# The depthwise convolution on TensorE: two 64-row units a tile, or sets of four 32-row matmuls

## What is computed

```
def conformer_conv_module(h, w_pw1, b_pw1, w_dw, b_dw, ln_g, ln_b, w_pw2, b_pw2):
    a = jnp.einsum("bsd,de->bse", h, w_pw1) + b_pw1
    u = a[..., :d] * jax.nn.sigmoid(a[..., d:])
    u = causal_dwconv(u, w_dw, b_dw)
    u = jax.nn.silu(layernorm(u, ln_g, ln_b))
    return jnp.einsum("bsd,de->bse", u, w_pw2) + b_pw2
```

## Time and profile before

| | us |
|---|---|
| median of 3 runs (949.39 to 950.07) | 949.61 |
| the profiled execution | 950.07 |
| its span | 948.3 |
| TensorE busy in it | 938.4 |
| VectorE busy | 552.4 |
| ScalarE busy | 393.4 |
| POOL busy | 112.2 |

### The profile page before, as it was taken

How to read it: one execution, slowest core, us unless ns; L and a number is a source line. 1 busy time by engine, 2 the same in 40 slices (tenths; PEclk the granted TensorE clock), 3 DMA queues, 4 the chain that set the end, 5 groups by cost and what they waited for, 6 DMA issues and landing times.

```text
span 948.3 us, 11921 instructions
## 1 busy us (share of the span) xinstructions
PE 938.4 (99%) x4512; PEld 791.2 (83%) x4512; DVE 552.4 (58%) x703; ACT 393.4 (41%) x606; POOL 112.2 (12%) x74
## 2 busy tenths in 40 slices
PE   8999999999999999999999999999999999999997
PEld 6889899888888888888888898888888888888887
DVE  6899995657555555555434359765555655532333
ACT  7785596434333333332222355433333333322231
POOL 0558896000000000000000020000000000000000
PEclk9999999999999999999999999999999999999999
DMA  7320022233222222312232341233222232223212
GB/s 254 116 89 1 1 90 89 90 99 110 102 88 88 88 88 97 123 63 91 76 107 91 117 147 55 89 108 113 88 88 88 88 94 100 64 90 122 91 62 90
DMA packets 17020, 88.56 MB, mean 93 GB/s; under 512 B 2016, under 2 KB 4320, under 8 KB 9952
## 3 DMA queue, kind: packets, MB, share of 16 engines
q1 hardware_dynamic: 16416, 87.67, 27.2%
q10 hardware_dynamic: 576, 0.52, 0.2%
HBM read 86.09 MB, written 2.10 MB: 93 GB/s over the span
## 4 chain that ended last, share of the span: by engine, by line
PE 97%; DMA 1%; SPq 1%; DVE 0%; ACT 0%; issue 0%; DVEq 0%
PE bank L1138 29%; PE bank L1139 29%; PE bank L1140 29%; PE bank L1190 2%; PE bank L1191 2%; PE bank L1189 2%; DMA w_raw<-w_pw 1%; PE bank L1480 1%; PE bank L1224 1%; PE bank L1207 0%; PE bank L1448 0%; PE bank L1453 0%; PE bank L1452 0%; PE bank L1213 0%; PE bank L1342 0%; SPq L302 0%
## 5 line engine op out<-in xcount | busy, mean ns | idle before, releaser
L1138 PE MATMUL bank<-h_hi,w_hi 128*128 128x512 f32 x800 | 312.4, 390 | 1.4 <-DVE w_lo L768 1.4
L1140 PE MATMUL bank<-h_hi,w_lo 128*128 128x512 f32 x800 | 311.3, 389 | 0.0
L1139 PE MATMUL bank<-h_lo,w_hi 128*128 128x512 f32 x800 | 311.2, 389 | 0.0
L455 ACT ACTIVATE w_hi<-w_raw 128x2048 fp32r<-128x2048 f32 (+2 forms) x87 | 147.3, 1693 | 214.3 <-PE bank L1140 214.3
L768 DVE TENSOR_TENSOR w_lo<-w_raw,w_hi 128x2048 fp32r<-128x2048 f32 (+2 forms) x81 | 162.2, 2002 | 100.7 <-ACT w_hi L455 100.0
L1138 PEld LDWEIGHTS bank<-h_hi,w_hi 128*128 128x128 f32 x800 | 150.2, 188 | 33.5 <-DVE w_lo L768 1.8
L1139 PEld LDWEIGHTS bank<-h_lo,w_hi 128*128 128x128 f32 x800 | 150.2, 188 | 31.7 <-issue 0.5
L1140 PEld LDWEIGHTS bank<-h_hi,w_lo 128*128 128x128 f32 x800 | 150.2, 188 | 30.8
L1139 PE MATMUL bank<-u_lo,w_hi 128*128 128x512 f32 (+1 forms) x406 | 153.3, 378 | 0.0
L1138 PE MATMUL bank<-u_hi,w_hi 128*128 128x512 f32 (+1 forms) x374 | 141.0, 377 | 0.0
L1140 PE MATMUL bank<-u_hi,w_lo 128*128 128x512 f32 (+1 forms) x374 | 140.8, 377 | 0.0
(11 more groups left out here) (212 smaller groups left out, 1001.3 us busy)
## 6 DMA issues: line engine op xcount, KB each, us to landing
w_raw<-w_up SPq DMA_DIRECT2D x44, 1024.0 KB, 4.8
w_raw<-w_down SPq DMA_DIRECT2D x32, 704.0 KB, 4.0
w_raw<-w_pw SPq DMA_DIRECT2D x11, 1024.0 KB, 4.9
x_res<-x SPq DMA_DIRECT2D x3, 512.0 KB, 7.7
out<-out_sb SPq DMA_DIRECT2D x12, 128.0 KB, 1.9
w_raw<-w_pw SPq DMA_DIRECT2D x4, 256.0 KB, 7.7
w_raw<-w_pool SPq DMA_DIRECT2D x2, 512.0 KB, 3.7
band_raw<-band SPq DMA_DIRECT2D x1, 800.0 KB, 5.4
```

Source lines behind the costliest of these rows:

```text
L455: nc.scalar.activation(w_hi[s][:, 0:columns], w_raw[s][:, 0:columns], ACT.Copy).then_inc(w_rounded[s], 1)
L1138: M.matmul(dst, a, hi, start=start, stop=False)
L1139: M.matmul(dst, a, lo, start=False, stop=False)
L1140: return M.matmul(dst, b, hi, start=False, stop=stop)
```

## The change

Each of the four TensorE tiles is now convolved by matmuls that use 32 rows of the array each. A set is four of them, one for each quarter of the 128 channels (`quad(q)`), each into a PSUM bank of its own. The 128 output rows are 2 phases of the tokens (`PHASES`) x 2 shares of the filter (`PARTS_OF_TAPS`: taps 0 to 15 and 16 to 30) x 32 channels. A tile is 17 offsets x 3 passes x 4 matmuls of 32 rows, 128 output rows and 264 columns: 204 matmuls (`conv_tile`). Before it was 96 of 128x256.

The result has the channels of a quarter and the shares of the filter on other partitions than `conv_out` wants. ScalarE copies the four banks to a staging tile with the bias (`drain_conv`), 16 DMAs of 32 partitions x 1 KB bring them to two summands (`gather`: by SP, and for tiles 6 and 7 half of them by ScalarE's own queue), and POOL adds these (`add_parts`).

With it: the gate's unit comes first in each step of the projection and the value's second; VectorE takes no tap of tile 6 and drains no tile 7; the near mean is subtracted from VectorE's accumulators ahead of tap 20 (`centre_sums`); the building of blocks is 32 ScalarE instructions and 4 POOL ones in all; the tile order on TensorE is step 2, tile 2, the gate's unit of step 3, tile 3, the value's unit of step 3, tile 6, tile 7; all sums of the norm but three are behind tile 7, with 34 matmuls of ones among them.

```diff
-CONV_UNITS = 2 * len(CONV_TILES)
-SHIFTS = (TAPS + 1) // 2
-HALF_CH = P // 2
-EVEN = (PAD + T) // 2
...
+QUADS = 4
+QUAD = P // QUADS
+PHASES, PARTS_OF_TAPS = 2, 2
+HALF_TAPS = (TAPS + 1) // 2
+OFFSETS = HALF_TAPS + PHASES - 1
+ENTRIES = (OFFSETS + PHASES - 1) * PARTS_OF_TAPS
+SPAN = (PAD + T + 2) // PHASES
+TP = T // PHASES
+LAG = HALF_TAPS // PHASES
...
-BANKS_PW1 = [(0, 2), (6, 0), (2, 6), (2, 6)]
-BANKS_CONV = (0, 0, 1, 1, 0, 0, 1, 0)
+BANKS_PW1 = [(0, 2), (6, 0), (2, 6), (6, 6)]
...
+        def gather(queue, n, q):
+            for p in range(PHASES):
+                for h in range(PARTS_OF_TAPS):
+                    queue.dma_start(gathered[n][quad(q), h, PHASES - 1 - p, :], stage[n][quad(PARTS_OF_TAPS * p + h), q, LAG * h:LAG * h + TP]).then_inc(part_gathered[n], 16)
...
+            load_step(w_pw2, 0, M_PW2, UNIT)
+            for n in range(len(CONV_TILES)):
+                for q in range(QUADS if n < 2 else QUADS // 2):
+                    sp.wait_ge(even_drained, QUADS * n + q + 1)
+                    gather(sp, n, q)
...
+            def add_parts(n):
+                pool.wait_ge(part_gathered[n], 16 * QUADS * PHASES * PARTS_OF_TAPS)
+                nc.gpsimd.tensor_tensor(by_phase(conv_out[:, CONV_TILES[n], :]), gathered[n][:, 0, :, :], gathered[n][:, 1, :, :], ADD).then_inc(conv_added, 1)
...
+            split(0, M_PW2)
+            pool.wait_ge(near_copied, 1)
+            for c in range(3):
+                nc.gpsimd.tensor_tensor(conv_out[:, c, :], conv_out[:, c, :], near_mean, SUB).then_inc(dev_early, 1)
             split_even(2)
             split_even(3)
...
+            add_square(1)
+            add_square(2)
+            split(1, M_PW2)
+            add_parts(1)
+            pool.wait_ge(conv_added, 2)
+            nc.gpsimd.tensor_tensor(conv_out[:, 3, :], conv_out[:, 3, :], near_mean, SUB).then_inc(dev_early, 1)
+            add_square(3)
+            add_parts(2)
+            pool.wait_ge(conv_added, 3)
+            nc.gpsimd.tensor_tensor(conv_out[:, 6, :], conv_out[:, 6, :], near_mean, SUB).then_inc(dev_sixth, 1)
+            add_parts(3)
...
-                c = CONV_TILES[n]
-                act.wait_ge(conv_done, 2 * n + 2)
-                for g in range(2):
-                    for p in range(2):
-                        bias = (col("b_dw", c) if p == g else bias_other[:, n:n + 1])[half_rows(p), :]
-                        nc.scalar.activation(conv_out[half_rows(g), c, p:T:2], bank[BANKS_CONV[2 * n + g]][half_rows(p), g * HT:(g + 1) * HT], ACT.Identity, bias=bias).then_inc(even_drained, 1)
+                act.wait_ge(conv_done, n + 1)
+                if n in (1, 3):
+                    act.wait_ge(part_gathered[n - 1 - n // 3], 16 * QUADS * PHASES * PARTS_OF_TAPS)
+                for q in range(QUADS):
+                    nc.scalar.activation(stage[n][:, q, :], bank[BANKS_CONV[n][q]][:, 0:TP + LAG], ACT.Identity, bias=bias_out[:, q, n:n + 1]).then_inc(even_drained, 1)
+                if n >= 2:
+                    for q in range(QUADS // 2, QUADS):
+                        act.wait_ge(even_drained, QUADS * n + q + 1)
+                        gather(act, n, q)
...
+            drain_conv(1)
+            act.wait_ge(near_mm, 1)
+            nc.scalar.activation(near_mean, bank[BANK_MEAN][:, :], ACT.Copy).then_inc(near_copied, 1)
+            act.wait_ge(unit_done[1], M_PW1 + PW1_STEPS)
+            for c in range(3):
+                act.wait_ge(dev_early, c + 1)
+                square_dev(c)
...
+            touch_root()
             drain_conv(2)
-            act.wait_ge(conv_done, 6)
-            round_unit(0, M_PW2, UNIT)
-            act.wait_ge(dev_late, 1)
-            nc.scalar.activation(bank[BANK_REST][:, :], conv_out[:, 4, :], ACT.Copy).then_inc(rest_added, 1)
-            touch_root()
-            square_dev(4, bank[BANK_SQUARES])
-            act.wait_ge(dev_late, 2)
-            square_dev(5, dev_sq[:, 5, :])
-            act.wait_ge(dev_late, 3)
-            square_dev(6, dev_sq[:, 6, :])
...
+            def centre_sums():
+
+                dve.wait_ge(near_copied, 1)
+                for t in range(2):
+                    acc = bank[BANKS_ACC[t]][:, :]
+                    dve.wait_ge(tap_step[t], TAPS + CENTRED_AT)
+                    V.tensor_tensor(acc, acc, near_mean, SUB).then_inc(tap_step[t], 1)
...
             multiply(0)
-            taps(0, 0, 8)
+            taps(0, 0, 4)
+            drain_gate(1)
+            taps(0, 4, 8)
-            taps(0, 8, 13)
-            drain_gate(1)
-            taps(0, 13, 15)
             multiply(1)
-            taps(0, 15, 20)
+            taps(0, 8, 14)
+            drain_gate(2)
+            taps(0, 14, 21)
-            taps(0, 20, 24)
-            drain_gate(2)
-            taps(0, 24, 26)
             multiply(2)
-            taps(0, 26)
-            taps(1, 0, 8)
+            taps(0, 21)
+            taps(1, 0, 2)
+            drain_gate(3)
+            taps(1, 2, 14)
-            taps(1, 8, 15)
-            drain_gate(3)
-            taps(1, 15, 16)
             multiply(3)
-            taps(1, 16, 24)
-            taps(1, 24 + 2 * SHARED_SHIFTS)
+            taps(1, 14, CENTRED_AT)
+            centre_sums()
+            taps(1, CENTRED_AT, TAPS - 1)
+            dve.wait_ge(conv_added, 4)
+            V.tensor_tensor(conv_out[:, 7, :], conv_out[:, 7, :], near_mean, SUB).then_inc(dev_last, 1)
+            taps(1, TAPS - 1)
...
-            def conv_unit(u, between=None):
-                n, g = u // 2, u % 2
-                if u in BUILT_BY_ACT:
-                    pe.wait_ge(hi_by_act, BUILT_BY_ACT.index(u) + 1)
-                else:
-                    pe.wait_ge(hi_by_pool, BUILT_BY_POOL.index(u) + 1)
-                pe.wait_ge(lo_built, u + 1)
-                pe.wait_ge(even_rounded, 4 * n + 4)
-                pe.wait_ge(even_crossed, 2 * n + 2)
-                if n < 2:
-                    wait_drained((2, 3), DRAINED_PW1 + 2)
-                else:
-                    pe.wait_ge(even_drained, 12 if u == CONV_UNITS - 1 else 4 * (n - 2) + 4)
-                dst = bank[BANKS_CONV[u]][:, g * HT:(g + 1) * HT]
-                first = SHARED_SHIFTS if CONV_TILES[n] == SHARED_TILE else 0
-                for k in range(first, SHIFTS):
-                    hi, lo = (x[:, 3 * n + 2 * g, k:k + HT] for x in (even_hi, even_lo))
-                    a, b = conv_hi[u][:, k * P:(k + 1) * P], conv_lo[u][:, k * P:(k + 1) * P]
-                    M.matmul(dst, a, hi, start=k == first, stop=False, skip_group_check=True)
-                    M.matmul(dst, a, lo, start=False, stop=False, skip_group_check=True)
-                    last = M.matmul(dst, b, hi, start=False, stop=k == SHIFTS - 1, skip_group_check=True)
-                    if between:
-                        between(k)
+            def conv_tile(n):
+                pe.wait_ge(hi_built, 1)
+                pe.wait_ge(lo_built, n + 1)
+                pe.wait_ge(even_rounded, n + 1)
+                pe.wait_ge(even_split, n + 1)
+                for m in range(OFFSETS):
+                    at_block = slice(n * ENTRIES + m * PARTS_OF_TAPS, n * ENTRIES + (m + PHASES) * PARTS_OF_TAPS)
+                    for w, x, first, final in ((block_hi, even_hi, m == 0, False), (block_hi, even_lo, False, False), (block_lo, even_hi, False, m == OFFSETS - 1)):
+                        for q in range(QUADS):
+                            last = M.matmul(bank[BANKS_CONV[n][q]][:, 0:TP + LAG], flat(w[quad(q), at_block, :]), x[quad(q), n, m % PHASES, m // PHASES:m // PHASES + TP + LAG], start=first, stop=final, skip_group_check=True)
                 last.then_inc(conv_done, 1)
...
+            pw1_unit(0, 1)
+            for i in (1, 2):
+                for s in range(2):
+                    pw1_unit(i, s)
+            wait_drained((2, 3), DRAINED_PW1 + 3)
+            for t in range(2):
+                pe.wait_ge(glu_done[t], 2)
+            conv_tile(0)
+            pw1_unit(3, 0)
+            pe.wait_ge(even_drained, QUADS)
+            conv_tile(1)
+            pw1_unit(3, 1)
+            pe.wait_ge(near_copied, 1)
+            conv_tile(2)
+            for t in range(2):
+                pe.wait_ge(glu_done[t], PW1_STEPS)
+            pe.wait_ge(even_drained, 2 * QUADS + 2)
+            conv_tile(3)
+            pe.wait_ge(even_drained, 3 * QUADS)
+            keep_busy(10, BANK_DEV)
+            pe.wait_ge(even_drained, 4 * QUADS)
+            keep_busy(4, BANK_WARM)
+            pe.wait_ge(dev_early, 4)
+            sum_wide(conv_out[:, 3, :], start=True, stop=False, at_bank=BANK_DEV)
+            keep_busy(2, BANK_WARM)
+            pe.wait_ge(squares_early, 3)
+            sum_wide(dev_sq[:, 0, :], start=True, stop=False, at_bank=BANK_DEV_SQ)
+            keep_busy(4, BANK_WARM)
+            pe.wait_ge(dev_sixth, 1)
+            sum_wide(conv_out[:, 6, :], start=False, stop=False, at_bank=BANK_DEV)
+            keep_busy(4, BANK_WARM)
```

(50 more changed lines are left out.)

330 lines of the change are left out of this document (111 added, 219 removed).

## The result

| us | before | after |
|---|---|---|
| median of 3 runs | 949.61 | 956.58 (955.11 to 956.70) |
| the profiled execution's span | 948.3 | 954.8 |
| TensorE busy in it | 938.4 | 936.2 |
| the variance's first instruction | 147.78 | 153.89 |

The ratio of after to before is 1.0064 (95% interval 1.005 to 1.0078): slower by 0.6%. The forecast was 948.2, with a range to 956.0. The point that the forecast chose for its sum, the variance on VectorE, is 6.1 us later than in the earlier trace rows and the span is 6.5 us longer, so nearly all of the loss lies ahead of it, as the forecast assumed.

What follows compares the result with a forecast made beforehand. TensorE, busy 99% of the span, was taken as the bound, with the change worth what it moves the variance: 1.6 us gained less 0.2 for changes of matmul kind, net -1.4 from 949.61, so 948.2; range 945.6 to 956.

Steps and rivals of the forecast that it cites:

- C: Time of one new tile on TensorE, 51 sets of four 32-row matmuls: taken as 0.122 us a set, 6.2 us.
- R1: Rival, chance 0.15: sets cost more than a full matmul, 0.161 us each, tile 8.2 us; +5.8 us, 955.4.
- R2: Rival, chance 0.09: the four 32-row matmuls do not overlap at all, tile 22.4 us; +62.6 us, 1012.
- Steps 1 to 3: Up to the last product: block building costs nothing, VectorE idles 4.4 us, VectorE reaches `scale_val(3)` at 111.9, TensorE 111.1.
- Step 4: New wait ahead of tile 6 for the last product and POOL's split: TensorE idle 5.0 us, tile 6 starts at 116.1.
- Step 5: Tile 6 ends at 122.3; tile 7 waits 1.1 us for two bank copies and runs from 123.4 to 129.6.
- R3: Rival, chance 0.13: the clock falls in the 5 us wait ahead of tile 6, 1.8 us extra; +0.4, 950.0.
- Step 6: Behind tile 7: TensorE's ones and sums take 16.5 us, to 146.1; the DMA path, to 140.0, is hidden by 0.8.
- Step 7: Variance starts at 146.2 instead of 147.8, 1.6 us gained, net -1.4; SP's gathers ahead of the weight loads cost nothing.
- R5: Rival, chance 0.07: gathers land later than 2 us, each us beyond 0.8 paid in full; 4 us give 949.4.

## Why the prediction was wrong, point by point

*C, the unknown, was right.* Forecast 0.122 a set and 6.2 us a tile; measured 0.12 and 6.3 (of 6.45, with the change of kind). One after the other 204 matmuls at 0.122 would be 24.9 us (an estimate; no run has them so), and by it four run 24.9 / 6.3 = 3.95 times as fast. With it R1 and R2 fell. (R1's turning point of 6.7 is 6.8 by its own sum, 4 x 0.6 - 0.8 = 1.6; nothing hung on it.) The Trainium skill ("TensorE: Matmul & The Clock Gate", Part 3) gives 3.07 for four tiles of 32 rows, measured there with 512 columns. This trace differs, and by its number tile 2 would have taken 8.1 us.

*Steps 1 to 3 were right to 2 us.* VectorE waited 4.3 at `scale_val(1)` (4.4 forecast). Both engines arrived late together: unit (3, 1) ended at 112.9 instead of 111.1 and `scale_val(3)` began at 112.92 instead of 111.9. Of the 1.8, 1.6 are small change on TensorE: 0.25 at the start of tile 2, 0.25 for each of two tiles by the change of kind (6.45 and 6.47), 0.2 for each unit (11.1 from 83.20 to 94.32), and 0.87 for the near sum instead of 0.4.

*Step 4, the wait*, was 4.55 us (5.0), and tile 6 started at 117.43 instead of 116.1: +1.3.

*Step 5 failed by the clock*: 8.9 us for tile 6 instead of 6.2, +2.7, and 0.25 more around tile 7. This is R3, which had 1.8 and a chance of 0.13. "The longest wait inside this trace is 1.4 us" was no ground for a low chance: it said that the trace held no case. The only row for the price, the kernel's first matmuls, allowed up to 3.2, and 2.7 lies near that end. (The profile gives 1.00 as the granted clock there, so that row was read as a slow clock from the matmuls' times alone.) The Trainium skill ("TensorE: Matmul & The Clock Gate", "HAM oscillation — how this bites in real kernels") has waits of a few us halve the clock; here the wait of 4.55 did.

*Step 6, the DMA path*, was "hidden by 0.8 us and no more". In the forecast it ran 8.4 us from tile 7's end to the landing; it ran 12.2. From tile 7's end to the last gather's issue it took 6.6 instead of 5.9: ScalarE was still issuing tile 6's gathers when tile 7 ended (eight in 6.4 us, one of them 1.42 long) and ran nothing else meanwhile, and a square stood behind them, so its copies of tile 7 began 0.8 behind tile 7's end. The forecast had taken 0.54 an issue from the larger stores of the earlier trace rows. From issue to landing it took 5.56 instead of 0.54 + 2.0: +3.0. So the subtraction ended at 148.1 instead of 140.0: 4.25 + 0.7 + 3.0 = 8.0.

*Step 7 is the step that failed in its logic*, in its last sentence, which priced SP's early loads at nothing; the runs put 2.7 us (profile) to 4.2 us (medians) in its place. "SP is through at about 134 where the old order issued that load at 143, so this costs nothing." It asked whether the loads come too late, and never what they do to the gathers when they come too early. The kernel before has no gather that a load could delay, so its trace could not price this; but the forecast's own times held the meeting: SP free at 134, ScalarE's last gather issued by 136. R5 had the right effect, a landing of over 2 us, but looked for its cause in the gathers' small packets. The trace's answer on the gathers, over all 64 of them, shows by its median of 1.9 us that these cost nothing by themselves:

```profile
DMA to landing us min/median/max: 1.8/1.9/5.6
```

*The sum closed.* At the variance: tile 7's end +4.25, the ones and sums to the last wait +0.4, the wait for the subtraction 2.67, the six sums behind it 5.6 instead of 5.3, +0.3. That is 7.6 of the measured 7.7 (146.2 to 153.89). No other term is needed for this execution. Against the kernel before, the forecast's gain of 1.6 at this point (147.78 to 146.2) became a loss of 6.1.

*What the two causes leave over.* With both removed and the tail as forecast the kernel is at 951.65. So of the 8.4 us between 948.2 and 956.58 the clock and the collision together carry 4.9 in medians. Of the other 3.5, 1.9 are small terms like those above (at the variance, in the trace), and 0.9 is the distance of the median of ten from the profiled execution, the fastest; 0.7 stays open.

*The range* reached 956.0. It took the rivals one at a time. R3 and R5 together, which is what happened, were in no case of it, though nothing in the profile made them exclude each other: one makes the tile late and the other its transfer.

What stays open: holding the loads gains 4.2 us in medians where the profile shows 2.7 for it, and keeping the clock gains 0.6 to 1.1 where profiles show 1.45 to 3.1. The clock comes back at different moments in different executions (ScalarE's copy of tile 6 begins 125.06 to 126.42). A median of four or five runs doesn't tell these shares apart better.

## What to carry to other kernels

Price a small transfer by what is issued beside it at that moment on any queue, and ask of a load that moves forward what it overtakes. A cover of less than a microsecond behind three engines and a DMA was none here: work that needs nothing late belongs ahead of the last arrival, and that order was worth 2.8 us together with the ten ones that it let go. A new wait of several microseconds on TensorE has to be costed with the slower clock behind it, or filled, and matmuls of ones that look idle may be what holds the clock: without its 34 behind tile 7 this kernel lost another 2.6 us.

## What the runs showed of the hardware

- Four fp32r matmuls of 32 rows with 264 columns, each with its own weights, go every 0.12 us at a granted clock of 1.00 and every 0.22 at 0.50. At 1.00 they do so whether the neighbours in the program use different rows or the same.
- With three passes of one quarter next to each other in the program, the first passes of all four quarters still started together (76.25 in that trace): matmuls on different rows did not start in the program's order.
- With 4.55 us without a matmul the granted clock fell to 0.50. In the kernel after it fell within the wait, near 116, and stayed there through 5 us of dense 32-row matmuls, to 122.8. In the one with held loads the same wait had it at 0.50 from 118 to 121 only. With ones in the wait it stayed at 1.00.
- A gather of 32 KB inside SBUF lands in 1.9 us in the median of 64, and in 5.35 to 5.73 when two loads of 1 MB are issued 0.3 us ahead of it on another queue (five executions). Behind one load on its own queue it lands about when the load does: after 4.8 us when issued 0.4 behind it, after 2.4 when issued 4.2 behind it.
- While both queues issued tile 6's gathers (127 to 134) the slowest landed in 3.4 us, with no load beside it. The runs don't show why.
- An issue of such a gather held ScalarE for 0.63 to 0.99 us on average, by kernel and tile, against 0.54 for the stores of 128 KB in the earlier trace rows.
